# Reordering the last pair of heads: two banks for the dense pieces, the value branch and the decays earlier, row and inverse transfers at new places in the queue

## The reference

```python
y_a = spatial_gating(u, v, ...) @ w_pa          # gelu(u) * (w_s mixed over tokens with layernorm(gelu(v))) + bias
y_b = gdn_output(o_gdn, z, ...) @ w_pb          # gated delta rule, 8 heads, forwards and backwards
y   = (sigmoid(gate_a) * y_a + sigmoid(gate_b) * y_b) @ w_out
```

## Time and profile before

| | |
|---|---|
| median of 3 runs | 1061.7 us (1061.43 to 1061.73) |
| profiled execution, first to last instruction | 1062.4 us |
| PE busy | 894.9 us (84%) |
| DVE busy | 647.0 us (61%) |
| ACT busy | 520.6 us (49%) |
| POOL busy | 177.6 us (17%) |
| last pair, from `scores(0)` to the last `level_turn` | 519.6 to 617.1 us of the span |

### The profile page before, as it was taken

The page is one execution under the profiler, slowest core; times in us unless marked ns, Lnnn a source line. Parts: engine busy times, 40 slices in busy tenths (PEclk is TensorE's granted clock), DMA queues, the critical chain, the costliest instruction groups (busy, mean ns, idle before and its releaser), DMA issues. The chain is left out here.

```text
span 1062.4 us, 14126 instructions
## 1 busy us (share of the span) xinstructions
PE 894.9 (84%) x5494; PEld 760.4 (72%) x5494; DVE 647.0 (61%) x837; ACT 520.6 (49%) x832; POOL 177.6 (17%) x323
## 2 busy tenths in 40 slices
PE   2899888988789987899776898994999999999991
PEld 0578777888668876688676787873778777778771
DVE  1277466443754447545346444757798887888774
ACT  2366542324523246332463222544777777877761
POOL 3102050012500124001204001001121111111002
PEclk9899989999899998999988899996999999999996
DMA  8555447431483315843444552691799999999984
GB/s 292 192 162 166 126 93 214 125 94 48 109 250 106 90 45 134 219 138 90 144 124 137 170 174 67 218 338 40 264 356 358 392 363 374 387 378 381 362 303 139
DMA packets 218893, 216.79 MB, mean 204 GB/s; under 512 B 33168, under 2 KB 154681, under 8 KB 218185
## 3 DMA queue, kind: packets, MB, share of 16 engines
q1 hardware_dynamic: 216089, 205.90, 59.8%
q0 software_dynamic: 2736, 9.96, 2.5%
HBM read 194.83 MB, written 21.00 MB: 203 GB/s over the span
## 5 line engine op out<-in xcount | busy, mean ns | idle before, releaser
L1907 DVE TENSOR_TENSOR w_lo<-raw,w_hi 128x2048 fp32r<-128x2048 f32 x96 | 222.9, 2330 | 48.6 <-ACT w_hi L1378 48.1
L2124 PE MATMUL bank<-hT,half_hi 128*128 128x256 f32 (+1 forms) x1024 | 235.4, 326 | 16.6 <-ACT staged L1075 13.1
L1378 ACT CAST w_hi<-raw 128x2048 fp32r<-128x2048 f32 x96 | 183.2, 1911 | 74.7 <-DMA raw<-in_w_e_dram 68.0
L2124 PEld LDWEIGHTS bank<-hT,half_hi 128*128 128x128 f32 x1024 | 173.9, 199 | 33.3 <-ACT staged L1075 14.1
L1508 DVE TENSOR_TENSOR half_lo<-half_raw,half_hi 128x1024 fp32r<-128x1024 f32 x88 | 108.5, 1236 | 102.1 <-ACT half_hi L977 101.8
L2124 PE MATMUL bank<-lane 128*128 128x128 f32 (+1 forms) x1072 | 142.2, 293 | 25.3 <-DMA lane<-inverse 14.0
L2124 PE MATMUL bank<-hT,half_lo 128*128 128x256 f32 (+1 forms) x512 | 163.2, 319 | 0.0
L2124 PEld LDWEIGHTS bank<-lane 128*128 128x128 f32 (+1 forms) x1072 | 130.7, 200 | 37.1 <-issue 19.9
L2124 PE MATMUL bank<-w_hi,window 128*128 128x512 f32 x480 | 155.3, 395 | 0.0
L2124 PEld LDWEIGHTS bank<-hT,half_lo 128*128 128x128 f32 x512 | 101.5, 198 | 5.9
L2124 PEld LDWEIGHTS bank<-w_hi,window 128*128 128x128 f32 x480 | 90.1, 188 | 19.2
(11 more groups left out here) (302 smaller groups left out, 1294.5 us busy)
## 6 DMA issues: line engine op xcount, KB each, us to landing
raw<-in_w_e_dram SPq DMA_DIRECT2D x96, 1024.0 KB, 7.9
half_raw<-in_w_in_dram SPq DMA_DIRECT2D x64, 512.0 KB, 4.2
half_raw<-in_w_ada_dram SPq DMA_DIRECT2D x32, 512.0 KB, 4.2
raw<-in_w_ada_dram SPq DMA_DIRECT2D x8, 1024.0 KB, 10.1
expert_rows<-y_out POOLq DMA_DIRECT2D x15, 512.0 KB, 7.7
dense<-staged SPq DMA_DIRECT2D x32, 128.0 KB, 3.0
lane<-inverse SPq DMA_DIRECT2D x16, 256.0 KB, 5.4
lane<-inverse_turned SPq DMA_DIRECT2D x16, 256.0 KB, 4.7
```

What stands on the lines that cost most here:

```text
L1378: act.copy(e_hi[n % WBUF][:, :], raw[n % RING][:, :]).then_inc(s["hi_ready"], 1)
L1907: dve.tensor_tensor(e_lo[n % WBUF][:, :], raw[n % RING][:, :], e_hi[n % WBUF][:, :].bitcast(F32), ALU.subtract)\
L2124: return nc.tensor.matmul(dst, lhsT, rhs, start=start, stop=stop)
```

## The change

Only the lists of the last pair change, with the banks that they use. Dense pieces with odd numbers above 24 go to bank 2 and even ones stay in bank 3, so that a piece waits for the copy of the last piece but one. `branch_a` alternates banks 0 and 1 where it had bank 2 alone. On PE `turn_mix` comes before `scores(3)`, `mix` comes after `dense(30)`, `branch_a(1)` stands between `level_p(0)` and `level_up(0)`, `ada_chunk(6)` ahead of `level_p(1)`, and `branch_a(2)` ahead of `level_up(1)`. On ACT the four `decay_exp` and the two `intra_exp` all stand ahead of `gelus(v_gelu)`. On DVE `sgu` comes after the split of PA1. On SP `move_rows` and `move_blocks` come earlier, `move_solved` and `move_inverse` come before the spills of pieces 29 and 30, and `load_gate_a` comes last, behind `move_inverse`.

```diff
@@ -458,6 +458,9 @@
 
         def two(t):
             return t[:, :].rearrange("p (c n) -> p c n", c=2)
+
+        def dense_bank(n):
+            return bank[2 if n > 24 and n % 2 else 3][:, 0:256]
 
         def spills_in(b, count):
 
@@ -678,27 +681,27 @@
             load_u()
             after_split(DENSE_AT[24])
             spill(24)
+            move_rows(0, 3)
+            move_rows(3, 4)
             after_split(DENSE_AT[25])
+            move_blocks()
             spill(25)
-            move_rows(0, 3)
             after_split(DENSE_AT[26])
-            move_rows(3, 4)
             spill(26)
-            move_blocks()
             after_split(DENSE_AT[27])
+            load_bias()
             spill(27)
             after_split(DENSE_AT[28])
-            load_bias()
             spill(28)
             after_split(DENSE_AT[29])
+            move_solved()
             spill(29)
             after_split(DENSE_AT[30])
+            move_inverse()
             spill(30)
-            move_solved()
             after_split(DENSE_AT[31])
+            spill(31)
             load_gate_a()
-            spill(31)
-            move_inverse()
             after_split(PA_AT[0])
             after_split(PA_AT[1])
             after_ada(6)
@@ -1072,7 +1075,7 @@
                 act.wait_ge(s["half_used"], DENSE_AT[k] + 1)
                 if k >= STAGES:
                     act.wait_ge(spilled[k % STAGES], 16 * (k // STAGES))
-                act.copy(staged[k % STAGES][:, :], bank[3][:, 0:256]).then_inc(s["side_copied"], 1)
+                act.copy(staged[k % STAGES][:, :], dense_bank(k)).then_inc(s["side_copied"], 1)
 
             def decay_exp(g):
                 act.wait_ge(s["scores_ready"], i * 4 + (g + 1))
@@ -1286,33 +1289,33 @@
             i = PAIRS - 1
             o_scale(PAIRS - 2)
             decay_exp(0)
+            decay_exp(1)
             ahead(DENSE_AT[24])
-            decay_exp(1)
             decay_exp(2)
             dense_copy(24)
+            mix_copies()
+            decay_exp(3)
             ahead(DENSE_AT[25])
-            decay_exp(3)
+            intra_exp(2)
+            intra_exp(3)
             dense_copy(25)
+            ahead(DENSE_AT[26])
             gelus(v_gelu, "landed_v")
-            ahead(DENSE_AT[26])
-            mix_copies()
+            o_mul(PAIRS - 2)
             dense_copy(26)
             ahead(DENSE_AT[27])
-            intra_exp(2)
-            intra_exp(3)
-            o_mul(PAIRS - 2)
             dense_copy(27)
+            ahead(DENSE_AT[28])
+            gelus(u_gelu, "landed_u")
             o_high(PAIRS - 2)
-            gelus(u_gelu, "landed_u")
-            ahead(DENSE_AT[28])
             dense_copy(28)
             ahead(DENSE_AT[29])
             dense_copy(29)
             ahead(DENSE_AT[30])
-            sgu_high()
             dense_copy(30)
             ahead(DENSE_AT[31])
             dense_copy(31)
+            sgu_high()
             gate_tanh(gate_a, "landed_ga")
             ahead(PA_AT[0])
             ahead(PA_AT[1])
@@ -1690,6 +1693,7 @@
             def v_normal():
                 dve.wait_ge(s["v_power"], 1)
                 dve.wait_ge(s["mix_copied"], 2)
+                dve.wait_ge(s["o_gated"], PAIRS - 1)
                 for t in range(2):
                     for n in range(2):
                         ins = dve.tensor_scalar(v_ln[:, t, n * N:n * N + N], bank[MIX_BANK[2 * t + n]][:, :], ln_mv[:, t, 0:1],
@@ -1725,7 +1729,7 @@
                 if m == 0:
                     dve.wait_ge(s["branch_acted"], 3)
                 dve.scalar_tensor_tensor(out=gate_a[:, m, :], in0=gate_a[:, m, :], scalar=1.0,
-                                         in1=bank[2][:, 0:256], op0=ALU.add, op1=ALU.mult)\
+                                         in1=bank[m % 2][:, 0:256], op0=ALU.add, op1=ALU.mult)\
                     .then_inc(s["branch_a_ready"], 1)
 
             def branch_b(m):
@@ -1836,26 +1840,26 @@
                 step_out(3)
                 pair_out()
             i = PAIRS - 1
-            ahead(DENSE_AT[24])
             first_level(0)
             first_level(1)
-            ahead(DENSE_AT[25])
+            ahead(DENSE_AT[24])
             first_level(2)
             first_level(3)
+            ahead(DENSE_AT[25])
+            intra_mask(2)
+            intra_mask(3)
             ahead(DENSE_AT[26])
             ahead(DENSE_AT[27])
-            intra_mask(2)
-            intra_mask(3)
             v_stats()
             o_gate(PAIRS - 2)
-            o_low(PAIRS - 2)
             ahead(DENSE_AT[28])
             v_normal()
+            o_low(PAIRS - 2)
             ahead(DENSE_AT[29])
             ahead(DENSE_AT[30])
+            ahead(DENSE_AT[31])
             sgu()
             sgu_low()
-            ahead(DENSE_AT[31])
             ahead(PA_AT[0])
             masks(0)
             branch_a(0)
@@ -2220,7 +2224,12 @@
                 side(SIDE_AT["z", j, h], Z_AT[j, h]).then_inc(s["half_used"], 1)
 
             def dense(k):
-                side(SIDE_AT["dense", k], DENSE_AT[k]).then_inc(s["half_used"], 1)
+                c = SIDE_AT["dense", k]
+                if k > 24:
+                    pe.wait_ge(s["side_copied"], c - 1)
+                    latents(dense_bank(k), DENSE_AT[k], hT_hi[:, :, CTX:], hT_lo[:, :, CTX:]).then_inc(s["half_used"], 1)
+                else:
+                    side(c, DENSE_AT[k]).then_inc(s["half_used"], 1)
 
             def turn_channels(n):
                 tiles = TILES if n < 4 else 2
@@ -2405,9 +2414,9 @@
             def branch_a(m):
                 if m == 0:
                     pe.wait_ge(s["sgu_split"], 4)
-                if m:
-                    pe.wait_ge(s["branch_a_ready"], m)
-                latents(bank[2][:, 0:256], PA_AT[m], sgu_hi, sgu_lo).then_inc(s["half_used"], 1)
+                if m >= 2:
+                    pe.wait_ge(s["branch_a_ready"], m - 1)
+                latents(bank[m % 2][:, 0:256], PA_AT[m], sgu_hi, sgu_lo).then_inc(s["half_used"], 1)
 
             def branch_b(m, first, last):
                 dst = bank[2 + m % 4][:, 0:256]
@@ -2575,31 +2584,31 @@
                 intra_sum(3)
             i = PAIRS - 1
             scores(0)
+            scores(1)
             dense(24)
-            scores(1)
             scores(2)
+            turn_mix()
+            scores(3)
             dense(25)
-            scores(3)
             dense(26)
-            turn_mix()
             turn_v(0)
             dense(27)
             turn_v(1)
             turn_out(PAIRS - 2)
             dense(28)
             dense(29)
+            dense(30)
             mix()
-            dense(30)
             dense(31)
             branch_a(0)
             level_p(0)
+            branch_a(1)
             level_up(0)
-            branch_a(1)
             level_turn(0)
+            ada_chunk(6)
             level_p(1)
-            ada_chunk(6)
+            branch_a(2)
             level_up(1)
-            branch_a(2)
             ada_fold(6)
             level_turn(1)
             level_p(2)
```

## The result

The change made the kernel slower: the median of 20 runs is 1070.0 us (1061.8 to 1078.4), that of 20 runs of the kernel before 1064.7 us (1057.1 to 1075.2). The ratio is 1.0059, with a 95% interval of 1.0031 to 1.0087. Ratios here leave out executions more than 1.5% above the fastest of their kernel (one of e1's took 2243 us), while medians are of all. The forecast was 1061.2 us, no change that can be measured, with a range up to 1063.8. Of the 8.8 us between forecast and result, 3.0 us are the kernel before itself, whose median is 1064.7 and not the 1061.7 of its first three runs.

A forecast was written before the change was run, and what follows sets the result against it. Bound by waits between engines, three chains meeting at 577 to 591: masks(0) 0.7 us earlier, the path to level_turn(1) 0.2 longer, so 0.5 earlier; 1061.9 from the span, 1061.2 as median, range 1058.8 to 1063.8.

The forecast's parts named there:

- early blocks bought nothing: POOL: inverse blocks landing near 542, some 12 us earlier, gain nothing, since v_norm stands ahead of solve_blocks.
- the wait moved into `ada_chunk(6)`: PE: ada_chunk(6), now ahead of level_p(1), waits for c3, issued after PA3's split; PE idles 3 us.
- `gate_a` landed after 589: Load of gate_a: a sign that would show the forecast wrong; the forecast had it land at 586.2.
- M: Start of masks(0) on DVE: forecast at 590.3 instead of 591.0, 0.7 us earlier.
- from `v_norm` to the end of the solve: POOL: 17.4 us, taken from the old trace, putting the solve's end at 566.3.
- the landing of `gate_a`: Load of gate_a behind the inverse: 6.2 us from issue at 580.0 to landing at 586.2.
- the queue: SP: eight inverse issues take 7.25 us, then two spills and c1, so gate_a is issued at 580.0.
- the clock in `ada_chunk(6)`: PE: low clock after 3 us of idling costs 0.7 us, chosen between nothing and 2.1.
- (a): Rival: gate_a does not hold back the level, masks(0) follow level_p(0), 11.5 us earlier, time 1050.4; chance 0.06.
- (c): Rival: gate_a served behind 2 MB of inverse, load takes 8.5 us, time 1064.0; chance 0.15.
- (d): Rival: transfers move but nothing else does, v_norm on POOL stays at 554.8, time 1067; chance 0.02.
- Costed at nothing: ACT's two dropped table loads (1.28 us each), two dense banks (copy some 0.5), rows ahead of pieces on SP: no effect.

The follow-up runs named there:

- e1: Changed kernel with the load of gate_a issued ahead of the eight inverse loads instead of behind them: median 1062.1 us, ratio to before 0.9986.
- e2: Changed kernel with ada_chunk(6) put back behind level_p(1) on PE: median 1065.4 us, ratio to before 1.0001.
- e3: Changed kernel with gate_a loaded ahead of the inverse and ada_chunk(6) back behind level_p(1): median 1055.6 us, ratio to before 0.991.
- e7: Changed kernel with PA2 and PA3 rounded and split early, DVE's branch_a(0) behind updates(0), ada_chunk(6) behind level_p(1), v_norm inside the solve: 1046.2 us, ratio to before 0.9869.
- e4: Changed kernel with ACT rounding PA2 and PA3 ahead of gate_a's tanh and DVE's branch_a(0) behind updates(0): median 1060.6 us, ratio to before 0.9962.
- e5: Changed kernel with VectorE's remainders of five pieces made for 64 columns only, part of the computation left out: single run, 1063.4 us.
- e6: Changed kernel with v_norm after the ninth of the solve's fifteen steps on POOL instead of ahead of it: median 1056.7 us, ratio to before 0.9932.
- e8: Kernel before with ACT rounding PA2 and PA3 ahead of gate_a's tanh and DVE's branch_a(0) behind updates(0): median 1067.4 us, ratio to before 1.0059.

## Why the prediction was wrong, step by step

**The mechanism held, and so did most of the signs that the prediction named.** Gating branch and inverse both came earlier; early blocks bought nothing; `gate_a` behind the inverse set the masks; the wait moved into `ada_chunk(6)`. The fixed pieces measured as they were read: end of the solve to the first inverse load 5.0 us (5.0), first inverse load to `gate_a` 8.4 (8.6), tanh to masks 4.0 (4.1), mask to the second half of the chunk 12.7 (12.4). DVE idled 24.4 us before PA2's split (20), PE 5.4 and 3.2 us in its two stalls (5 and 3). That was the structure; the sizes at its two ends were off. By one of the prediction's own signs (`gate_a` landed after 589) it was wrong: reckoned from the same `scores(0)`, ACT's tanh started on it at 591.8. `level_turn(1)` was forecast 96.9 us into the stage and came at 104.9, 8.0 late, 5.5 from the first step below and 2.5 from the second.

**The step that failed first was the sum up to M.** I had M 0.7 us earlier than before. From `scores(0)` it was 70.7 forecast, 76.2 measured, 5.5 late. The terms: `v_norm` at 31.1 instead of 29.3, 1.8 late, of which some 1.1 belongs to the execution (where the first matmuls of `scores(0)` take 1.19 us, as in after, e2, e3 and e7, it is at 31.1, and where they take 0.68, as in e1, e4, e5 and e6, at 29.9 to 30.1); from `v_norm` to the end of the solve 20.4 instead of 17.4, 3.0 late; the landing of `gate_a` 7.3 instead of 6.2, 1.1 late; the queue 0.2 early. So about 4.4 of the 5.5 are terms that I had too small, and 1.1 is a scatter that I couldn't have known from one trace.

The 3.0 is the largest, and it is the term that I took unchanged from the trace: 17.4 us from `v_norm` to the end of the solve. The sum had itself put `sgu` at 559.2 to 569.2 and the solve at 548.9 to 566.3, more of the one beside the other than before, and gave that overlap no price. These are long steps of POOL, and what DVE ran beside them, in the kernel before:

```profile
560.24 1.29 POOL L847 TENSOR_TENSOR lane<-lane 128x55 f32<-128x55 f32 x1
...
564.32 2.37 POOL L847 TENSOR_TENSOR lane<-lane 128x63 f32<-128x63 f32 x1
```

```profile
560.15 1.23 DVE L1508 TENSOR_TENSOR half_lo<-half_raw,half_hi 128x1024 fp32r<-128x1024 f32 x1 [3.47 <-ACT half_hi L977]
...
564.17 2.35 DVE L1508 TENSOR_TENSOR half_lo<-half_raw,half_hi 128x1024 fp32r<-128x1024 f32 x2
```

In the change, besides the step of 3.01 us at 557.25 shown above:

```profile
561.48 1.29 POOL L850 TENSOR_TENSOR lane<-lane 128x60 f32<-128x60 f32 x1
...
565.15 0.78 POOL L850 TENSOR_TENSOR lane<-lane 128x63 f32<-128x63 f32 x1
...
571.85 0.54 POOL L850 TENSOR_TENSOR lane<-lane 128x15 f32<-128x15 f32 x1
```

```profile
565.07 0.69 DVE L1715 TENSOR_TENSOR u_gelu<-u_gelu,mixed 128x512 f32<-128x512 f32 x1
...
569.72 2.60 DVE L1724 TENSOR_TENSOR sgu_lo<-u_gelu,sgu_hi 128x512 fp32r<-128x512 f32 x4 [0.68 <-ACT sgu_hi L1157]
```

Three remainders ran beside the solve in both kernels, and their two long steps together are 0.6 us longer in the change (4.30 against 3.66). The other 2.4 or so lie on steps beside the gating branch. In the change eight of them take 0.54 to 0.84 us instead of 0.2 to 0.35, four beside `sgu` and four beside `sgu_low`. Before there were two (0.67 and 0.57), as the solve ended during `sgu`, and `sgu_low` came behind it. So it is the gating branch, moved onto the solve, that made up most of this term. e5 shows that what DVE does beside the solve sets its length (13.5 us with the remainders thinned); the share of `sgu` is read from the steps of the two traces, and no run takes `sgu` off.

**The second was the clock in `ada_chunk(6)`.** From M to `level_turn(1)` I had 26.2, and it took 28.7. The stall was as long as forecast (3.22 us), but it cost more behind it: eight matmuls of the chunk took 1.93 instead of 0.96, and `level_p(1)` 5.90 instead of 3.74, 3.1 us in place of the 0.7 that I had chosen from bounds of 0 and 2.1. The upper bound came from a restart of two level products; here the chunk paid as well. The windows have 0.57 of the clock in 609 to 617. By the same reckoning the pause cost 1.6 to 1.8 us in e1, e4 and e6 and 3.0 in e5, so a price of 0.7 is too small everywhere and its size varies. The Trainium skill (TensorE: Matmul & The Clock Gate, Why this matters for your kernels) warns of pauses between bursts of matmuls for this reason, and the trace agrees: in e2, without the pause, `level_p(1)` takes 3.74.

**What this explains of the time.** The trace puts `level_turn(1)` 8.0 us later than the sum. Of the time itself 8.8 us were off: 3.0 by the median before and 5.8 by the change. The trace of the change is of an execution 7.6 us above its median, so its 8.0 may be more than a typical one loses; no second trace shows it.

**The rivals.** (a) is shown wrong by the trace after and by e4. (c) had the right sign and the right place, `gate_a` behind the inverse, but its price was put on the landing (8.5 us for 6.2); the landing took 7.3, and e1 shows what the place itself costs: 9.1 us of the stage, 1.0 of it `v_norm`. I had compared this place with the one before (0.9 gained) and so counted it as no loss, though against a transfer issued when ready it was the largest term. (d) is out too: `v_norm` came 4.1 us earlier. Its 1067 lies nearest to the measured 1070.0, but by luck.

**Costed at nothing.** Rows moved ahead of pieces held nothing up: ACT waited for the load of no piece between 520 and 575. The two banks of `branch_a` are of use, as e8 shows by their absence; those of the dense pieces were not tried by themselves. The two table loads fell out of ACT, and ACT then idled 22.59 us.

**The bound of measurement.** I took 0.2% for what can be told from no change. With the kernel's own scatter (1057 to 1075 us) 20 runs a side gave an interval of 0.28% to either side.

Not settled: how much of the 2.8 us in the expert stage of the profiled execution is more than scatter. The ten traces have 362.7 to 367.7 us from the first load of expert weights to the end, with no order.

## What to carry to other kernels

When a chain is made earlier, ask for each wait that used to end beside it what it waits for, and whether anything behind it in the same list needs that: here PA2's split and the masks stood behind a tanh that they don't need, which cost nothing while the inverse was late and put the masks 11.8 us later when it was not. Put a transfer that gates a long chain ahead of a bulk one in the queue, and take the order of work on engines that wait in vain before you take the order of transfers. Price a long run of small GpSimd steps by what VectorE does beside it after the change, not by its length in the old trace.

## What the runs showed of the hardware

- The solve, with its 30 small GpSimd steps, took 13.5 us with VectorE's remainders thinned (e5), 15.8 beside three 128x1024 remainders and a part of `sgu` (before), and 18.8 beside three remainders, `sgu` and `sgu_low` (after, e1, e2 and e3 alike). Single steps of 0.3 us took 3.0 (after) and 3.1 us (e6), ending right behind three instructions that VectorE ran back to back.
- In the change, GpSimd's steps beside `sgu`'s instruction that reads a PSUM bank (L1709, 564.16 to 565.04) kept their length (0.32 us at 564.37), while those beside its product of two SBUF tiles (L1715, 565.07) didn't (0.78 us at 565.15).
- After PE pauses of 3.1 to 3.2 us the next level product took 5.90, 4.39, 4.64, 5.74 and 4.72 us in five kernels of the same order (after, e1, e4, e5, e6) against 3.74 without the pause. e1 and e4 had run at the full clock for 9 us ahead of the pause, the others for 3 us, so that alone doesn't order them; what sets the price is open.
- Eight transfers of 256 KB took 6.4 us to issue in one queue after the change, 7.3 before, and 8.6 and 8.9 us in e1 and e3, with the 1 MB of `gate_a` just ahead of them.
